# The down projection's 64 sample rows computed for two column chunks together, on the two 64-column halves of the PE array

## What is computed

```python
def ffn_sublayer(h, prev, g, w_gu, conv_w, conv_b, w_down):
    gate, up = jnp.split(rms_norm(h, g) @ w_gu, 2, axis=-1)
    gate_c, state = causal_dwconv3(gate, prev, conv_w)
    return h + (jax.nn.silu(gate_c + conv_b) * up) @ w_down, state
```

## Time and profile before

| | us |
|---|---|
| device time, three runs | 1844.71, 1846.23, 1846.78 |
| median | 1846.23 |
| span of the profiled execution, first to last instruction | 1845.1 |
| first matmul of the down projection (from the span's start) | 1575.72 |
| last evacuation of the down projection begins | 1840.26 |

### The profile page before, as it was taken

One profiled execution on the slowest core, in us unless ns is written; L12 is line 12 of the kernel. 1 busy time (PEld: TensorE's weight loads), 2 busy tenths in 40 slices (PEclk: granted clock), 3 DMA queues, 4 the chain that ended last, 5 costly groups with the idle time before them and its releaser, 6 DMA issues.

```text
span 1845.1 us, 33734 instructions
## 1 busy us (share of the span) xinstructions
PE 1707.6 (93%) x13725; PEld 1187.0 (64%) x13803; DVE 1114.9 (60%) x1902; ACT 811.0 (44%) x1476; POOL 733.7 (40%) x704
## 2 busy tenths in 40 slices
PE   6999999996776899989887997999999999999998
PEld 3544445444444655545577544888888888899898
DVE  5856656787797764456655238888788787300000
ACT  5455688655435764432456226435444444110100
POOL 3232365987341200320023426666666666411200
PEclk9999999998797999999988998999999999999999
DMA  7031112023522110301344112121121222321211
GB/s 231 9 109 55 35 45 83 23 81 108 168 90 89 62 38 10 103 1 35 106 154 131 58 52 81 47 70 47 49 68 47 62 54 86 98 95 40 95 38 27
DMA packets 136548, 132.75 MB, mean 72 GB/s; under 512 B 15358, under 2 KB 109630, under 8 KB 136356
## 3 DMA queue, kind: packets, MB, share of 16 engines
q1 hardware_dynamic: 123850, 118.79, 20.7%
q10 hardware_dynamic: 12544, 11.80, 2.0%
HBM read 114.58 MB, written 15.98 MB: 71 GB/s over the span
## 4 chain that ended last, share of the span: by engine, by line
PE 71%; DVE 15%; ACT 6%; issue 4%; POOL 2%; DMA 2%; SPq 0%; ACTq 0%; DVEq 0%; POOLq 0%
PE PS L1558 23%; PE PS L1615 5%; PE PS L1616 5%; PE PS L1617 5%; PE PS L940 4%; PE PS L941 4%; PE PS L942 4%; ACT arena L1631 2%; PE PS L1104 2%; PE PS L1102 2%; PE PS L1103 2%; PE PS L1260 2%; ACT arena L1690 2%; PE PS L1272 1%; POOL arena L2964 1%
## 5 line engine op out<-in xcount | busy, mean ns | idle before, releaser
L1558 PE MATMUL PS<-arena 128*128 128x272 f16 (+1 forms) x3696 | 430.5, 280 | 5.0 <-issue 5.0
L1558 PEld LDWEIGHTS PS<-arena 128*128 128x128 f16 (+1 forms) x3696 | 362.5, 98 | 73.1 <-issue 5.4
L1631 ACT ACTIVATE arena<-PS 128x512 f16<-128x512 f32 (+11 forms) x381 | 189.9, 529 | 235.1 <-PE PS L942 81.3
L1631 ACT ACTIVATE arena<-arena 128x512 f16<-128x512 f32 (+5 forms) x214 | 136.3, 658 | 238.6 <-PE PS L1558 117.1
L368 POOL TENSOR_TENSOR arena<-arena 128x512 bf16<-128x512 f32 (+2 forms) x144 | 161.8, 1158 | 184.1 <-ACT arena L359 183.8
L940 PE MATMUL PS<-arena 128*128 128x512 f16 (+3 forms) x648 | 228.1, 362 | 5.2 <-DVE arena L2597 1.4
L941 PE MATMUL PS<-arena 128*128 128x512 f16 (+3 forms) x648 | 227.5, 361 | 0.0
L1615 PE MATMUL PS<-arena 128*128 128x256 f16 (+1 forms) x792 | 216.0, 273 | 1.4 <-POOL arena L918 1.0
L1617 PE MATMUL PS<-arena 128*128 128x256 bf16 (+1 forms) x792 | 215.9, 273 | 0.0
L1616 PE MATMUL PS<-arena 128*128 128x256 f16 (+1 forms) x792 | 215.9, 273 | 0.0
L942 PE MATMUL PS<-arena 128*128 128x512 bf16 (+2 forms) x608 | 212.0, 359 | 0.0
(11 more groups left out here) (351 smaller groups left out, 3693.6 us busy)
## 6 DMA issues: line engine op xcount, KB each, us to landing
arena<-w_gu SPq DMA_DIRECT2D x44, 512.0 KB, 4.8
arena<-w_down SPq DMA_DIRECT2D x8, 1408.0 KB, 7.8
arena<-w_in SPq DMA_DIRECT2D x8, 1024.0 KB, 5.1
arena<-w_kv_mem SPq DMA_DIRECT2D x8, 1024.0 KB, 7.2
arena<-cache_mem_k SPq DMA_DIRECT2D x32, 256.0 KB, 3.4
arena<-cache_mem_v ACTq DMA_DIRECT2D x28, 256.0 KB, 3.9
arena<-w_in SPq DMA_DIRECT2D x24, 256.0 KB, 3.8
arena<-x_prompt SPq DMA_DIRECT2D x9, 512.0 KB, 6.3
```

Of the source, the lines that this page charges most:

```text
L1558: mm = e.matmul(PS[:, product_bank(f, i) + c, 0:TC], w[:, i, k], s[i][:, q, c, :], start=first, stop=last)
L1631: e.activation(out, in_, ACT.Copy, **kw).then_inc(sem(name), 1)
```

## The change

The order of the tiles is now a list, `DOWN`. The four sample tiles (0, 8), (1, 8), (2, 8), (3, 8) become two: the tile written (0, 8) makes chunks 0 and 1, the tile written (2, 8) makes chunks 2 and 3. There are 34 tiles instead of 36, and the list ends with (3, 7). In such a tile chunk c goes to PSUM partitions 0 to 63 and chunk c + 1 to partitions 64 to 127 of the same bank, so the built program puts the first at array columns 0 to 63 and the second at columns 64 to 127. The matmuls of the two alternate. Their number is as before, 2 x 132 instead of 4 x 66, and so is their shape. The tile waits for both chunks' weights. Evacuation, residual loads and stores follow the list; the evacuation of such a tile covers 128 partitions, and it has two residual loads and two stores of 64 rows.

```diff
+        DOWN = [it for p in (0, 2) for it in [(p, j) for j in range(NB)] + [(p, NB)] + [(p + 1, j) for j in range(NB)]]
+        ND2 = len(DOWN)
+        DOWN_ENDS = [0, NT, NT + NB, 2 * NT + NB, ND2]
...
-        def down_store(e, c):
-            for j in range(NT):
-                n = c * NT + j
+        def down_store(e, first, end):
+            for n in range(first, end):
+                c, j = DOWN[n]
                 e.wait_ge(sem("down_ev"), n + 1)
...
+                    for g in range(2):
+                        e.dma_start(ys[:, (c + g) * 256:(c + g + 1) * 256], outb[g * NS:(g + 1) * NS, n % 4, :]
+                                    ).then_inc(sem(f"y_st{n % 4}"), 16)
...
-                down_store(e, c - 1)
-            down_store(e, 3)
+                down_store(e, DOWN_ENDS[c - 1], DOWN_ENDS[c])
+            down_store(e, DOWN_ENDS[3], ND2)
...
-                    out = PS[0:rows(j), 6 + n % 2, 0:256]
...
+            def down_samples(n, c):
+
+                sides = [(PS[g * NS:(g + 1) * NS, 6 + n % 2, 0:256], *down_weights(c + g)) for g in range(2)]
+                e.wait_ge(sem("dw_lo"), upto("dw_lo", lo_done(c + 1, 1)))
+                for k in range(FT):
+                    for out, wh, wl in sides:
+                        e.matmul(out, ffn_hi[:, k, SEQ:T], wh[:, k, :], start=(k == 0), stop=False)
+                    for out, wh, wl in sides:
+                        e.matmul(out, ffn_lo[:, k, SEQ:T], wh[:, k, :], start=False, stop=False)
+                    for out, wh, wl in sides:
+                        mm = e.matmul(out, ffn_hi[:, k, SEQ:T], wl[:, k, :], start=False, stop=(k == FT - 1))
+                mm.then_inc(sem("down_mm"), 1)
...
             def down_hi(c, half):
                 if c >= 2:
-                    e.wait_ge(sem("down_mm"), NT * (c - 1))
+
+                    e.wait_ge(sem("down_mm"), DOWN_ENDS[c - 1])
...
+                for g in range(down_moves(n)):
+                    e.dma_start(res[g * NS:g * NS + rows(j), n % 4, :],
+                                h3[j * P:j * P + rows(j), (c + g) * 256:(c + g + 1) * 256]
+                                ).then_inc(sem(f"res_ld{n % 4}"), 16)
...
-                e.tensor_tensor(outb[0:r, n % 4, :], PS[0:r, 6 + n % 2, 0:256], res[0:r, n % 4, :], ALU.add
+                e.tensor_tensor(outb[:, n % 4, :], PS[:, 6 + n % 2, 0:256], res[:, n % 4, :], ALU.add
                                 ).then_inc(sem("down_ev"), 1)
```

More of the change, by code:

```diff
@@ L639, in build, with down_moves, slot_moves @@
         FIRSTS, CONSTS = 2, 13
+        DOWN = [it for p in (0, 2) for it in [(p, j) for j in range(NB)] + [(p, NB)] + [(p + 1, j) for j in range(NB)]]
+        ND2 = len(DOWN)
+        DOWN_ENDS = [0, NT, NT + NB, 2 * NT + NB, ND2]
+        def down_moves(n):
+            return 2 if DOWN[n][1] == NB else 1
+        def slot_moves(n, k):
+            return 16 * sum(down_moves(m) for m in range(n) if m % 4 == k)
         def lo_done(c, half):
@@ L893, in _ @@
             for k in range(4):
-                e.wait_ge(sem(f"y_st{k}"), upto(f"y_st{k}", 16 * 9))
+                e.wait_ge(sem(f"y_st{k}"), upto(f"y_st{k}", slot_moves(ND2, k)))
             for k in range(2):
@@ L1593, in _ @@
                     product(f, i, (1,) if f == 0 and i in (M3, M4) else (0, 1)).then_inc(sem("gu_mm"), 1)
[L1595 to L1603, removed]
-                    out = PS[0:rows(j), 6 + n % 2, 0:256]
[L1605 to L1615, removed]
-                        e.matmul(out, ffn_lo[:, k, tcols(j)], wh[:, k, :], start=False, stop=False)
-                        mm = e.matmul(out, ffn_hi[:, k, tcols(j)], wl[:, k, :], start=False, stop=(k == FT - 1))
-                    mm.then_inc(sem("down_mm"), 1)
-                if c == 0:
@@ L1621, in _ @@
+            for n, (c, j) in enumerate(DOWN):
+                if n >= 2:
+                    e.wait_ge(sem("down_ev"), n - 1)
+                if n == 0:
+                    e.wait_ge(sem("fw_sum"), upto("fw_sum", 5 * FT))
+                if j < NB:
+                    down_tile(n, c, j)
+                else:
+                    down_samples(n, c)
+                if n == NB:
                     e.wait_ge(sem("f_mul"), FT)
@@ L2155, in _ @@
             copy(ffnst[:, 2560:DFF], PS[0:18, 5, 0:DFF - 2560], "ffnst_ev")
-            for n in range(NT + 2, 4 * NT):
+            for n in range(NT + 2, ND2):
                 if n == NT + 4:
```

33 lines of the change are left out of this document (24 added, 9 removed).

## The result

| | before | changed |
|---|---|---|
| median, first comparison (4 and 4 runs) | 1845.47 us | 1832.80 us (1829.88 to 1834.49) |
| ratio | | 0.9927, 95% interval 0.9914 to 0.9941 |
| ratio in two later comparisons | | 0.9906 (0.9889 to 0.9923) and 0.9929 (0.9916 to 0.9943) |
| span of the profiled execution | 1845.1 us | 1832.3 us |
| first matmul of the down projection | 1575.72 | 1577.96 |

The changed kernel is faster by 0.7% to 0.9% by the ratios, and by 12 to 18 us between the medians, according to the comparison. The last row of the table is the one that belongs to the change: 15.0 us.

What follows compares the result with a forecast made beforehand. The PE stream was taken to bound the down projection; 14.74 us saved less 0.1 us added gives 14.6 us, so 1846.2 - 14.6 = 1831.6, rounded to 1831.5 us. The range was 1829.5 to 1839.5 us.

Steps and rivals of the forecast that it cites:

- What bounds the kernel: In the down projection, from 1575.72 us to the end, the span is the PE stream and nothing else.
- Part 1: Two of the down projection's four sample tiles fall away, saving 7.41 and 7.33 us, together 14.74 us.
- Part 2: The two remaining sample tiles get 132 matmuls instead of 66; a pair costs 109 ns, adding 0.1 us in all.
- (a): A pair's two moving operands from the same 128 partitions fit: 5.9 columns per ns asked, some 6.5 seen in the attention.
- (b): In a sample tile's pair, 64-column weight loads take at most some 27 ns each, two of them 54, under 109.
- The smaller gain that was weighed: By the skill's figure, paired halves run 1.59 times as fast: sample tile 9.1 us, saving 10.8 us instead of 14.6.
- Part 3: What moves around the sample tiles costs nothing; GpSimd ends chunk 3's weights near 1727, 33 us ahead of need.
- The signs: Down projection's profile: tile (1, 0) near 1645, GpSimd done near 1727, last evacuation near 1825.6, sample tile some 7.4 us.
- No overlap: Rival: a sample tile's halves stream one after the other, 14.4 us a tile; 0.3 us saved, 1845.9 us; chance 0.11.
- The loads show: Rival: each sample-tile pair pays one or two 27 ns weight loads; 1835.2 to 1838.7 us; chance 0.08.
- a change of side waits: Slower rival: in sample tiles the other half's load waits for the matmul in flight; 1852 to 1871 us; chance 0.09.
- The slower rival's decision point: In the new sample tiles, a mean step from matmul to matmul over 110 ns turns the gain into a loss.

Runs made afterwards that it cites:

- narrow64: The changed kernel with each 256-column matmul of the sample tiles made as four of 64 columns; one time of 1845.28 us, the stage 260.55 us.
- blocks: The changed kernel with three matmuls of the left half, then three of the right, instead of left and right in turn; median 1830.90 us.
- serial: The changed kernel with all 66 left-half matmuls of a sample tile ahead of the 66 right-half ones; median 1845.31 us, 0.9985 to the kernel before.
- l8pair: The changed kernel plus the same pairing in the memory attention's output projection; medians 1827.53 and 1828.47 us, against 1830.24 and 1833.70 for the changed kernel.
- blocks12: The changed kernel with 12 matmuls of one half, then 12 of the other, in the sample tiles; one time of 1837.41 us, the stage 255.25 us.
- serial128: The kernel serial with sample-tile matmuls of 128 columns instead of 256; one time of 1844.43 us, the stage 263.38 us.

## Why the prediction was right, point by point

**What bounds the kernel.** Right for all that the change touches: the profile lists no wait of PE from 1630 us to the end, before or after. "The PE stream and nothing else" from 1575.72 on was a little too strong. Near its start the stage has two waits of PE, 1.0 us for GpSimd and 0.4 for VectorE. Both kernels have the same two, so they drop out of the difference.

**Part 1, two tiles that fall away, 14.74 us.** The stage became shorter by 14.73 us in the first trace and by up to 14.76 in the two others. That is the price of part 1 with part 2 at no cost.

**Part 2, what a pair costs.** The lower end was right: 109 ns, 3 to 4 of them between the two starts. The 0.1 us that I added for two tiles was not there. Of the two arguments, (a) held: two moving operands on the same 128 partitions cost nothing here. Argument (b) came to the right end but was too cautious in its mechanism: two loads were to fit one after the other in 54 ns, and in fact they run beside each other, 3 ns apart, even where a pair has 32 ns in all (`narrow64`).

**The smaller gain that was weighed.** The Trainium skill (TensorE: Matmul & The Clock Gate, "Measured speedup vs the span model") would by the estimate have left a pair at 1.59 times; it was 2.00 times over 66 pairs, 7.12 us for 132 matmuls against 7.12 for 66. The page's figure is for three tiles of 32 columns, a form that no run here has, so it is the estimate from it that failed. That page's rule in "The mechanism", that a weight load overlaps with matmuls in flight only when its row group differs, does not hold here: the two halves have the same rows, and the loads at 1637.50 start 0.03 us after matmuls of 0.30 us. Nor does its next sentence, that matmuls start and end in program order, as far as the starts go: in `blocks` and in the seams of `serial` matmuls of one half overtake those of the other. The ends are modelled in this profile and show nothing either way. The trace decides.

**Part 3.** Chunk 3's low parts were ready 33 us ahead of need, as worked out, with the load issued at 1705.88, which is 1703.6 once the 2.24 us are taken off by which this whole stage stood later. The one miss is the tail, which I left as it was: it is 0.28 us shorter, since the last store of a result and the one of `o_cfp` are issued faster (0.33 us for 0.47, and 0.29 for 0.44). Why they are was not looked into.

**The sum.** 14.6 expected; 15.0 in every trace of the changed kernel, the 0.1 that was not there and the 0.28 of the tail being the difference. The median of 1832.8 us lies 1.3 us above the 1831.5 predicted although the saving was larger, because the earlier stages scatter by several us from execution to execution. The range of 1829.5 to 1839.5 held it. The scatter of 0.2%, some 3.7 us, was put too low: fifteen later runs of the kernel before lie between 1843.83 and 1850.63 us. So that the median came within 1.3 us is in part luck, while the saving in the stage is not.

**The signs.** With 2.24 us taken off, tile (1, 0) starts at 1645.0, GpSimd is done at 1727.7 and the last evacuation starts at 1825.5, as written (1645, 1727, 1825.6). One sign was put down wrongly: from the full matmul ahead of a sample tile to the one behind it 7.53 us pass, not 7.4. It was 7.52 before, and the 7.41 of part 1 is that less one step.

**The rivals.** "No overlap" is what `serial` builds, but for its seams. Its price was 0.3 us under the kernel before; from the first matmul of the stage to the end of the span the trace has 1.4 us, which is the 0.3, some 0.8 of the two seams and the 0.3 of the tail. That its 1845.3 us stands so near the 1845.9 of the price is chance, since the kernel before had 1848.53 beside it. "The loads show" and "a change of side waits" did not occur: sides change 131 times a tile without a wait (the twelve row-half matmuls behind that argument change sides eleven times, not twelve). The slower rival's decision point, 110 ns a matmul, stands against 7.12 us / 131 = 54.4 measured.

## What to carry to other kernels

Where the stationary operand has 64 columns, two such products on the two column halves of the array cost what one costs (seen here with a contraction of 128 and moving operands of 256 and, in `l8pair`, 512 columns); look for every tile that has half a block of rows, and bring two of them together so that no more than three to six matmuls of one half stand in a row. Alternating strictly is not needed. Matmuls of 128 columns keep the gain but for 0.3 us in two tiles, while at 64 columns PE stopped again and again and most of the gain was lost (11.1 of 14.7 us). Read such a change in its own stage, from the first to the last start: here three comparisons put its worth at 12.2, 12.7 and 18.3 us between medians, while three traces gave 15.0.

## What the runs showed of the hardware that I had not expected

Matmuls of different column halves leave the order of the program. At a change of side four matmuls of the other half stream beside the last four of the run ahead of them, with 256 columns (seams of `serial`, `blocks12`) and with 128 (`serial128`) alike; runs of 3 hide wholly (249.50 us against 249.49), runs of 6 nearly (249.96), runs of 12 cost 5.8 us in two tiles.

Weight loads of 64 columns for the two halves run beside each other: a pair of loads and a pair of 64-column matmuls pass in 31 to 32 ns, and at the start of a tile two loads for each half take the step of 28 ns that two loads for one half take.

At four PE instructions in 32 ns PE stopped three times in 264 pairs, for 1.0 to 1.7 us from start to start; at four in 56 ns it did not stop. Each stop ended 1.35 to 1.46 us after a packet of 16,384 bytes on the instruction queue had landed, and 256 PE instructions lay between one stop and the next in a tile.
